# A decoder layer on one core: bf16 whole-number products in the expert listing, an unscaled turn of the second norm's rows, 41 expert steps in another order, and a third expert loaded early

## The chip, the cores and the metric

One core of one Trainium2 chip runs the whole layer. The metric is the device time of one execution in microseconds (us); the time of a kernel is the median of its runs. Engines: TensorE (PE; its weight loads are PEld), VectorE (DVE), ScalarE (ACT), GpSimd (POOL), SyncE (SP, which issues most DMAs). TensorE's granted clock is given as a share of 2.4 GHz.

## The reference

512 positions, width 1024, one layer. An attention part makes `h` (512 x 1024); then a mixture of experts is added:

```python
h = h + moe_ffn(rmsnorm(h, g_ffn), w_router, router_bias, w_gate, w_up, w_down, ws_gate, ws_up, ws_down)
# moe_ffn: scores = sigmoid(xf @ w_router); sel = scores + router_bias
#  the best 4 of 8 groups, then the best 8 of 64 experts by sel; w = scores of these, normalised, x 2.5
#  y[token] += w * ((silu(x @ w_gate[e]) * (x @ w_up[e])) @ w_down[e]) for each of its 8 experts
#  + (silu(xf @ ws_gate) * (xf @ ws_up)) @ ws_down      (the shared expert)
```

There are 64 experts with hidden width 256, so an expert's gate and up matrices are 2 MB in fp32 and its down matrix is 1 MB. 4096 (token, expert) pairs are computed. A gated embedding and a last norm follow. All tensors are fp32.

## The kernel before

Each engine has its own instruction stream, with semaphores between them written out by hand. The stages are `front_*` (input projection and attention), `middle_*` (merging, output projection, second norm, router, lists of rows), `experts_*` (the steps), `overflow_*` (a loop that runs only if an expert has more rows than its place) and `tail_*`.

**Middle.** TensorE makes the output projection in quarters of 256 columns for four tiles of 128 positions (`out_proj(t, q)`, L1100). When tile t's second half is added to `h` (L1278, counted by `h_done`), VectorE makes the sum of squares (`norm_sums`), GpSimd the power -0.5 (`rr`), and VectorE the normalised rows `y` (L1282, `xn`). `y` goes to DRAM as `xn2_rows` for the experts' gathers (L1024), and TensorE turns it (`transpose_xn`, L1111); VectorE and ScalarE each evict one half to `xn2T` (L1285, L1235). The router's products (L1119) and the shared expert's gate/up products (`shared_up`, L1125, eight of 512 columns a tile) read `xn2T`. ScalarE makes the scores (L1237). VectorE picks groups and experts (L1291 to L1328) and gives `mask`; then `wn`, the weights.

**Listing.** TensorE counts rows per expert with products of `mask` and ones (L1162, L1164), turns mask and weights (L1167, L1171), sorts experts by count with a permutation matrix (L1176, L1177, L1180), and gives each row its place by products with a triangle and ones (L1186) and an offset (L1191). All of these are fp32. The results are whole numbers, save the weights'. The weights are split into three bf16 parts by ScalarE and GpSimd in turns (L1245, L1248, L1043). `list_rows` (L963) are bf16 products of a one-hot matrix with a table `tokw`, which give each step's 128 row numbers and weights. Shared-expert products are put between these as filling.

**Steps.** Experts 0, 1 and 2 are fixed as ranks 0 to 2, so that they can be loaded before the order is known; the other ranks are sorted by row count. A step has 128 rows and is one of three kinds: F is one expert with 128 rows (`NFULL` of them, capacity 128); a trio T is two steps for two experts with 96 rows each and a third one with 32 rows in each; P is a pair with 64 rows each. The string `UNITS` gives their order; 42 steps. Step s on TensorE: gate/up products (L1484, 7 us), turning the next step's gathered rows (L1474), a list (L963), in the first steps one or two shared down products (L1071), the down products of step s-1 (L1508), and turning its own hidden rows (L1491). GpSimd gathers the rows of a step from DRAM and scatters its results.

**Loads.** There are six slots for experts' weights. `load_order` is ranks 0, 1, 2 and then the order of first use. A slot takes the next expert's gate/up as soon as the gate/up products of its holder's last step are done (semaphore `gu`), and its down matrix when the down products are done. The loads go out in SP's order (L1005, L1009). Before step 0, SP issues: experts 0 and 1 after the output projection, load 3 after the sorted `order`, gate/up of load 5, `w_shared_down`, and once all shared gate/up products are done, load 4, the rest of 5, and expert 2.

Of the kernel before, what the change touches and what calls it, by code (L numbers as in the profile page):

```python
# [21 lines left out]
BF16 = mybir.dt.bfloat16  # L22
ALU = mybir.AluOpType
# [26 lines left out]
NFULL = 6  # L50
NTRIO = 14
NPAIR = 8
# [52 lines left out]
def constants():  # L105
# [35 lines left out]
        ("cap_col", np.where(np.arange(P) % NE < NFULL, 128, np.where(np.arange(P) % NE < NFULL + 2 * NTRIO, 96, 64))[:, None]),  # L141
# [9 lines left out]
def build(nc, a, dbg=None):  # L151
# [8 lines left out]
    with ctx:  # L160
# [653 lines left out]
        wsg = sb("w_shared_up", X0, [P, 2, KD, EH])  # L814
# [4 lines left out]
        xpart = small[:, 96:104]  # L819

# [20 lines left out]
        UNITS = "FPPTTTPTFPTTTFTTFPPTPTTFPFTT"  # L841
        steps, n_full, n_trio, next_small = [], 0, 0, NFULL + 2 * NTRIO
        for u in UNITS:
            if u == "F":
                steps.append(full(n_full))
# [4 lines left out]
            else:  # L850
                steps += trio(NFULL + 2 * n_trio, NFULL + 2 * n_trio + 1, next_small)
# [13 lines left out]
        BUFFER = [2, 1, 0, 3, 4, 5]  # L865
        slot_of, landed_at, before, holder = {}, {}, {}, {}
        for x, r in enumerate(load_order):
# [3 lines left out]
            landed_at[r] = 16 + (landed_at[before[r]] if r in before else 0)  # L871
            slot_of[r], holder[v] = BUFFER[v], r

# [22 lines left out]
        sco, sel, selm, rep, mask, wn, pos1, smask = (wk(NT * NE, NT, NE) for _ in range(8))  # L896
# [5 lines left out]
        keys, above, perm = (wk(NE) for _ in range(3))  # L902
        own_key, my_rank = wk(1), wk(1)
        maskT, wnT = wk(NT * P, NT, P), wk(NT * P, NT, P)
# [10 lines left out]
        shared_in = {0: [(0, 0, 5), (0, 1, 6)], 1: [(1, 0, 7)], 2: [(1, 1, 7)], 3: [(2, 0, 7)], 4: [(2, 1, 7)], 5: [(3, 0, 7)], 6: [(3, 1, 7)]}  # L915
        shared_order = [v for i in range(7) for v in shared_in[i]]
# [15 lines left out]
        cn = ("sig merged_pe merged mt_hi mt_lo wo_done h_done ms rr xn stored xt_done xt_dve xt_act r_done listing_pe listing_act listing_dve listing_pool "  # L932
# [3 lines left out]
        for engine, done in (("pe", "counts maskT_pe wnT_pe sorted sorted_too pos_pe before_pe offs_pe"), ("act", "sco maskT wnT part0 part1 part2"),  # L936
                             ("pool", "rest0 rest1"), ("dve", "mask wn cnt_sb perm smask order over_pe over")):
# [73 lines left out]
        def middle_sync(sp):  # L1011
# [6 lines left out]
            for i, n in enumerate(("ws_gate", "ws_up")):  # L1018
                sp.dma_start(wsg[:, i], chunks(a[n][0])).then_inc(s_ws, 16)
# [41 lines left out]
        def shared_down(pe, t, i, b):  # L1061
# [6 lines left out]
            if n >= 2:  # L1068
# [1038 lines left out]
```

## Time and profile before

| | us |
|---|---|
| median of 3 runs | 1168.94 (1166.13 to 1172.79) |
| profiled execution | 1170.68 |
| its span | 1168.9 |
| TensorE busy | 1103.6 (94%) |
| VectorE busy | 462.8 (40%) |
| GB/s, mean over the span | 263 |

The span is the time from the first to the last instruction of the program. An idle stretch is put down to what ended it. Two records of TensorE belong to one fp32 product. The end of a matmul is modelled, so two records can overlap. A DMA's time to landing runs from its issue until all 16 of its parts have reported. All times below are us from the start of the span.

### The profile page before, as it was taken

To read this page: it belongs to the slowest core of one execution; us is meant where nothing else is said; L and a number is where in the kernel's file an instruction comes from. 1 tells how busy PE (TensorE), PEld (TensorE's weight loads), DVE (VectorE), ACT (ScalarE), POOL (GpSimd) and SP (SyncE) were. 2 spreads that over 40 slices of the span, in tenths; PEclk is the share of its full clock that TensorE was granted. 3 is DMA by queue.
4 is the path that set the end of the run, shared out by engine and by line. 5 is a ranking of instruction groups with operands and counts; after the bars stand their busy time and mean duration, and the time that the engine had idled before them with its cause. 6 is when DMAs were issued, how large, how long until landed. Compare 5 with 4: busy or idle time off the path is not lost.

```text
span 1168.9 us, 18877 instructions
## 1 busy us (share of the span) xinstructions
PE 1103.6 (94%) x7544; PEld 649.5 (56%) x7545; DVE 462.8 (40%) x1027; ACT 284.6 (24%) x642; POOL 283.4 (24%) x212
## 2 busy tenths in 40 slices
PE   6999999999998989999999999989998899998796
PEld 5888787767776879664333343334343333433375
DVE  5345655544546733542223422212221211111787
ACT  5023333333336410031111111111111111111623
POOL 3622524342333421010112112111111112110043
PEclk9999999999998989989999999999999999999899
DMA  9711212111112330669999999999999999988771
GB/s 365 266 37 37 73 55 73 54 55 55 55 38 104 130 119 37 250 235 411 404 424 414 424 425 427 421 419 421 412 422 417 427 399 421 425 360 316 321 313 72
DMA packets 51159, 307.77 MB, mean 263 GB/s; under 512 B 10368, under 2 KB 13312, under 8 KB 33152
## 3 DMA queue, kind: packets, MB, share of 16 engines
q1 hardware_dynamic: 38976, 272.99, 57.7%
q0 software_dynamic: 12096, 33.57, 7.2%
q8 instruction: 61, 1.00, 0.3%
q14 instruction: 26, 0.21, 0.0%
HBM read 290.80 MB, written 26.21 MB: 271 GB/s over the span
## 4 chain that ended last, share of the span: by engine, by line
PE 73%; DMA 16%; issue 5%; DVE 3%; POOLq 1%; POOL 1%; DVEq 0%; SPq 0%; ACT 0%
PE bank L1484 18%; PE bank L461 15%; DMA sb_gate_up<-in_w_gate_up 13%; PE bank L1508 8%; PE bank L1100 4%; PE bank L1090 4%; PE bank L470 3%; PE bank L494 3%; DMA sb_down<-in_w_down 3%; PE bank L525 3%; PE bank L1474 2%; PE bank L507 2%; PE bank L1125 2%; PE bank L1071 1%; PE bank L547 1%
## 5 line engine op out<-in xcount | busy, mean ns | idle before, releaser
L1484 PE MATMUL bank<-sb_gate_up,sb_xgT 128*32 128x512 f32 (+2 forms) x2144 | 301.8, 602 | 17.7 <-DMA sb_gate_up<-in_w_gate_up 17.7
L1484 PEld LDWEIGHTS bank<-sb_gate_up,sb_xgT 128*32 128x32 f32 (+2 forms) x2144 | 94.7, 118 | 192.7 <-issue 189.2
L461 PE MATMUL bank<-sb_x_hl,sb_w_hl 128*128 128x512 f32 x768 | 191.3, 401 | 10.6 <-DVE sb_x_hl L587 10.6
L461 PEld LDWEIGHTS bank<-sb_x_hl,sb_w_hl 128*128 128x128 f32 x768 | 141.7, 190 | 57.4 <-issue 24.5
L1508 PE MATMUL bank<-sb_down,sb_work 128*32 128x512 f32 (+2 forms) x1072 | 153.0, 595 | 3.9 <-DMA sb_down<-in_w_down 2.6
L1566 POOL DMA_INDIRECT expert_rows<-sb_rows_out,sb_work x42 | 43.6, 1037 | 455.3 <-DVE sb_rows_out L1644 455.3
L262 POOL TENSOR_TENSOR sb_w_hl<-sb_r,sb_w_hl 128x1024 fp32r<-128x1024 f32 x52 | 126.1, 2429 | 69.9 <-ACT sb_w_hl L1213 47.1
L1654 DVE TENSOR_TENSOR sb_work<-sb_work,bank 128x256 f32<-128x256 f32 x42 | 17.8, 423 | 269.4 <-ACT sb_work L1690 269.4
L1508 PEld LDWEIGHTS bank<-sb_down,sb_work 128*32 128x32 f32 (+2 forms) x1072 | 46.5, 116 | 80.3 <-issue 77.7
L1690 ACT ACTIVATE sb_work<-bank 128x256 f32<-128x256 f32 x42 | 16.2, 387 | 297.7 <-PE bank L1484 297.7
L671 DVE CUSTOM_DVE_ANT_0 sb_h<-bank,sb_bias 128x128 f32<-128x128 f32 (+3 forms) x96 | 43.4, 489 | 112.3 <-PE bank L494 111.7
L256 POOL CAST sb_w_hl<-sb_r 128x1024 fp32r<-128x1024 f32 x35 | 37.7, 1076 | 200.2 <-PE bank L461 157.6
L1644 DVE TENSOR_SCALAR sb_rows_out<-bank,sb_work 128x512 f32<-128x512 f32 x42 | 31.5, 751 | 134.9 <-PE bank L1508 134.9
L784 ACT ACTIVATE sb_h<-sb_h,sb_small 128x128 f32<-128x128 f32 (+3 forms) x96 | 53.3, 556 | 69.9 <-DVE sb_small L671 69.9
L1681 ACT ACTIVATE sb_rows_out<-bank,sb_work 128x512 f32<-128x512 f32 x42 | 28.9, 688 | 165.1 <-PE bank L1508 165.1
L794 ACT COPY sb_work<-bank 128x128 f32<-128x128 f32 (+4 forms) x104 | 40.5, 439 | 103.7 <-PE bank L507 92.9
L1474 PEld LDWEIGHTS bank<-sb_cst,sb_xg 128*128 128x128 f32 x336 | 41.0, 193 | 30.8 <-issue 29.1
L1100 PE MATMUL bank<-sb_w_hl,sb_m_hi 128*128 128x256 f32 x256 | 48.3, 291 | 4.8 <-DVE sb_m_lo L1258 4.8
L999 POOL DMA_INDIRECT sb_xg<-xn_rows,sb_work x42 | 43.4, 1033 | 37.9 <-PE bank L1474 16.4
L1474 PE MATMUL bank<-sb_cst,sb_xg 128*128 128x128 f32 x336 | 48.1, 286 | 0.0
L700 DVE TENSOR_SCALAR sb_h<-sb_h,sb_small 128x128 f32<-128x128 f32 (+3 forms) x96 | 43.3, 493 | 4.1 <-issue 0.4
L1100 PEld LDWEIGHTS bank<-sb_w_hl,sb_m_hi 128*128 128x128 f32 x256 | 41.3, 198 | 5.2 <-issue 5.2
(253 smaller groups left out, 1320.3 us busy)
## 6 DMA issues: line engine op xcount, KB each, us to landing
sb_gate_up<-in_w_gate_up SPq DMA_DIRECT2D x64, 2048.0 KB, 28.5
sb_down<-in_w_down SPq DMA_DIRECT2D x64, 1024.0 KB, 29.9
sb_r<-in_w_front SPq DMA_DIRECT2D x54, 512.0 KB, 3.5
sb_rows<-expert_rows SPq DMA_DIRECT2D x6, 2048.0 KB, 16.3
sb_gateT<-in_cmp_w SPq DMA_DIRECT2D x2, 2048.0 KB, 13.4
sb_rows<-expert_rows SPq DMA_DIRECT2D x3, 1024.0 KB, 8.5
sb_y<-in_x_T SPq DMA_DIRECT2D x4, 512.0 KB, 7.5
sb_h<-in_x SPq DMA_DIRECT2D x4, 512.0 KB, 11.1
```

The lines of the kernel that those rows point to most:

```text
L262: nc.gpsimd.tensor_tensor(w6_hl[:, slot, 1], raw_at[buf], w6_hl[:, slot, 0].bitcast(F32), ALU.subtract).then_inc(s_split, 1)
L461: last = nc.tensor.matmul(out[:, :], w6_hl[:, slot_at[n], zw, k, :], x_hl[:, zx, k, :], start=k + i == 0, stop=k == KD - 1 and i == 2)
L671: nc.vector.tensor_tensor_reduce(out=sc[:, i % 3, hh, 0:n_of(u)], in0=bank[BS[hh]][:, 0:n_of(u)], in1=bias[:, u["pair"] % 2, hh, S - n_of( ...
L700: nc.vector.tensor_scalar(sc[:, i % 3, hh, 0:n_of(u)], sc[:, i % 3, hh, 0:n_of(u)], c[:, hh:hh + 1], None, ALU.mult).then_inc(F["scaled"], 1)
L784: nc.scalar.activation(sc[:, i % 3, hh, 0:n_of(u)], sc[:, i % 3, hh, 0:n_of(u)], ACT.Exp, scale=-1.0, bias=minus_max[:, i % 4, hh:hh + 1], ...
L999: nc.gpsimd.indirect_dma_start(out=xg[s % 2], out_offset=None, in_=xn2_d, in_offset=bass.IndirectOffsetOnAxis(ap=idx[:, s:s + 1], axis=0), ...
L1090: last = nc.tensor.matmul(bank[2 * (m % 4) + i][:, :], w6_hl[:, SLOT_OF[m], zw, k, :], x_hl[:, zx, k, :], start=k % 4 + j == 0, stop=k % 4 ...
L1100: last = nc.tensor.matmul(bank[t][:, (q % 2) * 256:(q % 2 + 1) * 256], part_of_m, w6_hl[:, lo:lo + 2, zw, k, :], start=k + i == 0, stop=k ...
L1474: last = nc.tensor.transpose(bank[BX[half]][:, (k % 4) * P:(k % 4 + 1) * P], rows[:, k, :], ident)
L1484: last = nc.tensor.matmul(bank[BH][rows, :], xgT[:, k, rows], gate_up[slot_of[r]][:, :, k, :], start=k == 0, stop=k == KD - 1)
L1508: last = nc.tensor.matmul(bank[BO[i]][rows, :], hT[:, c, rows], Wd[slot_of[r]][:, c, i * 512:(i + 1) * 512], start=c == 0, stop=c == 1)
L1566: nc.gpsimd.indirect_dma_start(out=rows_d, out_offset=bass.IndirectOffsetOnAxis(ap=dst[:, s:s + 1], axis=0), in_=osb[s % 2], in_offset=Non ...
```

## The change

1. **bf16 for whole numbers.** `mask`, `smask`, `maskT`, `above`, `perm16`, `ones16`, `tri16`, `ident16`, `e_col16` are bf16; the products and the mask's transposes that read only these are bf16. `perm` stays in fp32 beside it for the weights and counts.
2. **Rows turned unscaled.** TensorE turns `h` instead of `y` (`transpose_h`), and one place earlier: after `out_proj(t + 1, 2)`. The gain `g_ffn` is multiplied in at the eviction, by columns (`g2_col`); the row factor `xpart` comes in later, as the scale of the sigmoid (now one operation per tile), of the shared SiLU, and of the product with the up half. The last tile's router product goes to a bank of its own. `y` is still made and stored for the gathers. The order of the shared products changes, and the copies to `tokw` move ahead of the residual adds. `ws_gate` and `ws_up` are one array, interleaved by chunk.
3. **Steps.** NFULL 1, NTRIO 17, NPAIR 6: 41 steps. The fixed experts have 96 rows in trios. The one expert with 128 rows is rank 3. The order begins T, P, P, P, P.
4. **Loads.** Expert 2 is loaded after the last W_out piece is split, ahead of the stores of the normalised rows. Loads 4 and 5 have their slots where `w_shared_up` and `xn2T` lie, and their gate/up weights come in two halves. One shared down product a step, in steps 0 to 7, all in bank 7.

```diff
-NFULL = 6
-NTRIO = 14
-NPAIR = 8
+NFULL = 1
+NTRIO = 17
+NPAIR = 6
+BIGGEST = NPRE
...
-        UNITS = "FPPTTTPTFPTTTFTTFPPTPTTFPFTT"
+        UNITS = "TPPPPTTTTTTTTTTPTTPTTFTT"
+        members = [r for r in range(NFULL + 2 * NTRIO) if r != BIGGEST]
...
-        BUFFER = [2, 1, 0, 3, 4, 5]
+        BUFFER = [1, 2, 3, 5, 0, 4]
+        IN_HALVES = (4, 5)
...
-        shared_in = {0: [(0, 0, 5), (0, 1, 6)], 1: [(1, 0, 7)], 2: [(1, 1, 7)], 3: [(2, 0, 7)], 4: [(2, 1, 7)], 5: [(3, 0, 7)], 6: [(3, 1, 7)]}
+        shared_in = {s: [(s // 2, s % 2, 7)] for s in range(2 * NT)}
...
             sp.dma_start(wsd[1][:, :], a["ws_down"][0, P:2 * P, :]).then_inc(s_wsd, 16)
+            sp.wait_ge(s_split, WO_PIECE + KD)
+            load_gate_up(sp, 2, 2)
+            load_down(sp, 2, 2)
...
-            def transpose_xn(t):
-                pe.wait_ge(M["xn"], t + 1)
+            def transpose_h(t):
+                pe.wait_ge(M["h_done"], NT + t + 1)
...
                 out_proj(t, 2)
+                if t:
+                    transpose_h(t - 1)
...
                 out_proj(t, 3)
-                if t:
-                    transpose_xn(t - 1)
-            pe.wait_ge(M["h_done"], NT + 1)
-            pe.wait_ge(s_ws, 32)
-            shared_up(0)
-            transpose_xn(3)
             router(2)
+            transpose_h(3)
+            pe.wait_ge(s_ws, 16)
+            shared_up(0, range(1))
             router(3)
+            shared_up(0, range(1, KD))
             pe.wait_ge(M["h_done"], 2 * NT)
-            shared_up(1)
-            shared_up(2, range(3))
+
+            others = [(t, k) for k in range(4) for t in range(1, NT)]
+            for t, k in others[:3]:
+                shared_up(t, (k,))
...
-                nc.tensor.matmul(bank[7][0:NE, 0:P], mask[:, t, :], C["ones"], start=t == 0, stop=t == NT - 1)
...
+                nc.tensor.matmul(bank[7][0:NE, 0:P], mask[:, t, :], ones16, start=t == 0, stop=t == NT - 1)
...
-                    last = nc.tensor.matmul(bank[6][:, t * NE:(t + 1) * NE], C["tri"] if v == t else C["ones"],
+                    last = nc.tensor.matmul(bank[6][:, t * NE:(t + 1) * NE], tri16 if v == t else ones16,
...
-            shared_up(2, range(3, 6))
+            for t, k in others[3:8]:
+                shared_up(t, (k,))
...
-            shared_up(2, range(6, KD))
-            shared_up(3)
+            for t, k in others[8:]:
+                shared_up(t, (k,))
+            for t in range(1, NT):
+                shared_up(t, range(4, KD))
...
-                nc.scalar.copy(xn2T[:, 4:8, t * P:(t + 1) * P], psv(5, 4, P)).then_inc(M["xt_act"], 1)
...
+                for k in range(4, KD):
+                    last = nc.scalar.activation(xn2T[:, k, t * P:(t + 1) * P], psv(5, 4, P)[:, k - 4, :], ACT.Copy, scale=g2_col[:, k:k + 1])
+                last.then_inc(M["xt_act"], 1)
...
-            sp.wait_ge(s_split, WO_PIECE + KD)
+            def half_of_gate_up(x, i):
+                slot = slot_of[load_order[x]]
+                sp.dma_start(raw[slot][:, i, :], a["w_gate_up"][expert[x]][:, 2048 * i:2048 * (i + 1)]).then_inc(s_raw[slot], 16)
+
+            sp.wait_ge(M["stored"], 16 * NT)
+            sp.wait_ge(M["xt_done"], NT)
             sp.wait_ge(*LISTING["order"])
             number(3)
             load_gate_up(sp, expert[3], load_order[3])
...
+            for x in IN_HALVES:
+                number(x)
+                load_down(sp, expert[x], load_order[x])
+            sp.wait_ge(M["gu_half"], 1)
+            for x in IN_HALVES:
+                half_of_gate_up(x, 0)
             sp.wait_ge(E["list"], 4)
             sp.dma_start(wsd[0][:, :], a["ws_down"][0, 0:P, :]).then_inc(s_wsd, 16)
+            load_down(sp, expert[3], load_order[3])
             sp.wait_ge(M["gu_done"], NT)
...
+            for x in IN_HALVES:
+                half_of_gate_up(x, 1)
```

## Rows read from the trace of the kernel before

**Rows 1.** The page's part 4: shares of the chain that ended last, by engine.

```profile
PE 73%; DMA 16%; issue 5%; DVE 3%; POOLq 1%; POOL 1%; DVEq 0%; SPq 0%; ACT 0%
```

**Rows 2.** Timeline of TensorE, 474 to 528: start, duration, line, form, records, [idle before].

```profile
474.41 7.03 PE L1125 MATMUL bank<-sb_w_shared_up,sb_gateT 128*128 128x512 f32 x16
...
482.15 3.68 PE L1119 MATMUL bank<-sb_gateT 128*128 128x64 f32 x32
...
495.50 1.09 PE L1162 MATMUL bank<-sb_cst,sb_work 128*64 128x128 f32 x8 [0.17 <-DVE sb_work L1328]
...
502.20 4.53 PE L1186 MATMUL bank<-sb_work,sb_cst 128*128 128x64 f32 x20
506.66 1.97 PE L1191 MATMUL bank<-sb_work 64*128 64x64 f32 x8
508.56 4.28 PE L1125 MATMUL bank<-sb_w_shared_up,sb_gateT 128*128 128x512 f32 x6
512.67 0.47 PE L963 MATMUL bank<-sb_work 128*128 128x6 bf16 x12
...
514.67 8.85 PE L1125 MATMUL bank<-sb_w_shared_up,sb_gateT 128*128 128x512 f32 x20
...
527.41 7.13 PE L1484 MATMUL bank<-sb_gate_up,sb_xgT 128*128 128x512 f32 x16
```

**Rows 3.** Windows: length, busy by engine, clock, DMA share, GB/s; sum over 474.40:527.40.

```profile
495.40:501.60 6.20, 5.41 (x43) 4.67 (x43) 3.60 (x15) 1.06 (x2) 0.00 (x0) 0.97 0.22 91
501.60:510.75 9.15, 9.15 (x34) 7.55 (x34) 3.26 (x6) 6.28 (x7) 1.70 (x2) 0.50 0.82 319
...
sum 53.00, PE 49.61 PEld 30.99 DVE 28.47 ACT 10.90 POOL 7.33; mean PE 6.20 PEld 3.87 DVE 3.56 ACT 1.36 POOL 0.92
...
552.40:1054.70 502.30, 481.52 (x3759) 187.31 (x3757) 112.60 (x249) 74.10 (x154) 79.43 (x77) 0.99 1.00 415
```

**Rows 4.** Waits of TensorE, 470 to 1100: total, times, longest.

```profile
PE bank L1484 <- DMA sb_gate_up<-in_w_gate_up: 17.7, 7, 4.0
...
PE bank L1508 <- DMA sb_down<-in_w_down: 2.6, 3, 1.3
```

**Rows 5.** The chain that ended last, in order of time: start, duration, what.

```profile
578.72 1.92 PE bank L1071 x4
...
627.13 7.00 PE bank L1484 x64
...
639.58 7.00 PE bank L1484 x64
...
1010.30 44.45 DMA sb_gate_up<-in_w_gate_up
...
1054.89 8.41 PE bank L1484 x64
```

**Rows 6.** Timeline of VectorE and ScalarE between scores and step 1.

```profile
486.29 0.43 DVE L1291 TENSOR_TENSOR sb_work<-sb_work,sb_gateT 128x256 f32<-128x256 f32 x1 [2.32 <-ACT sb_work L1237]
...
495.02 0.43 DVE L1328 TENSOR_TENSOR sb_work<-sb_work 128x256 f32<-128x256 f32 x1
...
507.21 1.36 ACT L1248 CAST sb_work<-sb_work 128x256 bf16<-128x256 f32 x1 [0.96 <-POOL sb_work L1043]
...
549.05 0.39 ACT L1690 ACTIVATE sb_work<-bank 128x256 f32<-128x256 f32 x1 [8.27 <-PE bank L1484]
```

**Rows 7.** Timeline of SP's queue: issues of expert loads.

```profile
502.13 0.35 SPq L1005 DMA_DIRECT2D sb_gate_up<-in_w_gate_up  x1
...
503.85 0.34 SPq L1005 DMA_DIRECT2D sb_gate_up<-in_w_gate_up  x1
...
534.72 0.35 SPq L1005 DMA_DIRECT2D sb_gate_up<-in_w_gate_up  x1
```

**Rows 8.** Line L1005: time to landing of the loads issued at 503.85 and at 534.72.

```profile
DMA to landing us min/median/max: 14.3/14.3/14.3
...
DMA to landing us min/median/max: 17.7/17.7/17.7
```

More of the change, by code:

```diff
@@ L819, in build @@
         xpart = small[:, 96:104]
+        g2_col = small[:, 436:436 + KD]
         m_hi = sb("m_hi", Y0, [P, NT, KD, P], F32R)
@@ L844, in build @@
             if u == "F":
-                steps.append(full(n_full))
+                steps.append(full(BIGGEST + n_full))
                 n_full += 1
@@ L850, in build @@
             else:
-                steps += trio(NFULL + 2 * n_trio, NFULL + 2 * n_trio + 1, next_small)
+                steps += trio(members[2 * n_trio], members[2 * n_trio + 1], next_small)
                 n_trio += 1
@@ L871, in build @@
             landed_at[r] = 16 + (landed_at[before[r]] if r in before else 0)
+            landed_gu[r] = (32 if x in IN_HALVES else 16) + (landed_gu[before[r]] if r in before else 0)
             slot_of[r], holder[v] = BUFFER[v], r
@@ L895, in build @@
         onehot_too = work[:, at_moe + NT * NE:at_moe + NT * NE + NT * CAP // 2].bitcast(BF16).rearrange("p (a b) -> p a b", a=NT)
-        sco, sel, selm, rep, mask, wn, pos1, smask = (wk(NT * NE, NT, NE) for _ in range(8))
+        sco, sel, selm, rep, wn, pos1 = (wk(NT * NE, NT, NE) for _ in range(6))
+        wk16 = lambda n: wk(n // 2).bitcast(BF16)
+        mask, smask = (wk16(NT * NE).rearrange("p (a b) -> p a b", a=NT) for _ in range(2))
+        ones16, tri16, ident16 = (wk16(P) for _ in range(3))
+        above, perm16, e_col16 = wk16(NE), wk16(NE), wk16(2)
         g8 = wk(NT * NG * 8, NT * NG, 8)
@@ L901, in build @@
         cnt_sb = wk(P)
-        keys, above, perm = (wk(NE) for _ in range(3))
+        keys, perm = (wk(NE) for _ in range(2))
         own_key, my_rank = wk(1), wk(1)
-        maskT, wnT = wk(NT * P, NT, P), wk(NT * P, NT, P)
+        wnT = wk(NT * P, NT, P)
+        maskT = wk16(NT * P).rearrange("p (a b) -> p a b", a=NT)
         assert at[0] <= WORK, at[0]
@@ L936, in build @@
         for engine, done in (("pe", "counts maskT_pe wnT_pe sorted sorted_too pos_pe before_pe offs_pe"), ("act", "sco maskT wnT part0 part1 part2"),
-                             ("pool", "rest0 rest1"), ("dve", "mask wn cnt_sb perm smask order over_pe over")):
+                             ("pool", "rest0 rest1"), ("dve", "mask wn cnt_sb perm perm32 smask order over_pe over")):
             for n, name in enumerate(done.split()):
@@ L1128, in shared_up @@
                     last.then_inc(M["gu_done"], 1)
+                elif (t, k) == (3, 3):
+                    last.then_inc(M["gu_half"], 1)
             pe.wait_ge(s_split, WO_PIECE + 4)
@@ L1232, in middle_scalar, with turned_rows @@
             round_piece(WO_PIECE + 7)
+            def turned_rows(t):
+                act.wait_ge(M["xt_done"], t + 1)
+                for k in range(4, KD):
+                    last = nc.scalar.activation(xn2T[:, k, t * P:(t + 1) * P], psv(5, 4, P)[:, k - 4, :], ACT.Copy, scale=g2_col[:, k:k + 1])
+                last.then_inc(M["xt_act"], 1)
+            act.wait_ge(s_g2, 32)
+            for t in range(NT - 1):
+                turned_rows(t)
+            turned_rows(NT - 1)
+            act.wait_ge(M["rr"], NT)
+            act.wait_ge(M["r_done"], NT - 1)
             for t in range(NT):
[L1234 to L1237 removed]
+                if t == NT - 1:
+                    act.wait_ge(M["r_done"], NT)
+                last = nc.scalar.activation(sco[:, t, :], router_out(t), ACT.Sigmoid, scale=xpart[:, 4 + t:5 + t])
+            last.then_inc(M["listing_act"], 1)
             act.wait_ge(*LISTING["maskT_pe"])
@@ L1271, in middle_vector @@
             dve.wait_ge(s_xagain, 16)
-            dve.wait_ge(s_g2, 16)
+            dve.wait_ge(s_g2, 32)
+            for v16, v in ((ones16, C["ones"]), (tri16, C["tri"]), (ident16, ident), (e_col16[:, 0:1], C["e_col"])):
+                nc.vector.tensor_copy(v16, v)
+            nc.vector.tensor_copy(tokw[:, :, :, 0], C["tok_a"].unsqueeze(1).to_broadcast([P, NE, NT]))
+            nc.vector.tensor_copy(tokw[:, :, :, 1], C["tok_b"].unsqueeze(1).to_broadcast([P, NE, NT]))
             for t in range(NT):
```

87 lines of the change are left out of this document (41 added, 46 removed).

## The prediction

> **What bounds the kernel now.** I read the page's shares first: TensorE is busy 94% of the span and 73% of the chain that ended last is its work, 16% is DMA [rows 1]. That average hides two stages. From about 474 to 527 us, routing and listing, the reader should see in TensorE's timeline one long file with small holes: whatever leaves it brings step 0 forward [rows 2]. From step 0 on the windows tell something else. Over 502 us the DMA engines have share 1.00 at 415 GB/s while TensorE is busy 481.52 of 502.30 [rows 3]. TensorE's waits in that stage are only 17.7 us for gate/up weights and 2.6 us for down weights [rows 4], so the two are nearly in step. Which one sets the end is told by the chain: the 63rd gate/up load is issued at 1010.30, lands 44.45 us later, at 1054.75, and step 40 begins 0.14 us after that [rows 5]. A load that lands 44 us after its issue stood in a queue; the 2 MB themselves take 5 us at 415 GB/s. So **the end is set by the stream of expert weights**: landing of load 63, then two steps and the tail, 1168.9 - 1054.75 = 114.2 us, none of which the change edits.
>
> The need of each kind of step says the same. One expert is 3.15 MB, and rows in and out are together 33.6 MB over 42 steps, 0.8 MB a step. Two steps of a trio (3 experts) need (9.44 + 1.6)/0.415 = 26.6 us of DMA against 2 x 12.45 = 24.9 us of TensorE; a pair step 17.1 against 12.45; a step of one full expert 9.5 against 12.45. All 64 experts and the rows: 235 MB/0.415 = 566 us of DMA, against 42 steps of TensorE = 42 x 12.45 + 8 x 1.8 = 537 us [rows 3, 5]. DMA is the longer by 29 us.
>
> **Change 1, 42 steps become 41.** One step is 12.45 us of TensorE (627.13 to 639.58) [rows 5]. The 4096 routed rows and 64 experts remain, so DMA has the same bytes. With the end set by the stream, this is worth **0**: TensorE waits 12 us more for weights. Were TensorE the bound it would be 12.4. I take 0, as the queue is 44 us long at the end. The last units are F, T, T in both orders, so load 63 still releases the last but one step. Going back from step 39: the F step waits for load 58, which is 5 experts and 3 steps' rows earlier, (15.7 + 2.4)/0.415 = 44 us against 37 us of steps, so load 63 decides; the trio before F waits for load 56, 63 us against 62, a tie; further back the stream's lead grows again. So at most a microsecond of the step's worth is near. For the capacities I counted the reference's routing on its own inputs: the fixed experts have 71, 56 and 67 rows (96 allowed), the largest other 102 (128), the next 88 (96), and from rank 35 on at most 62 (64). Nothing overflows.
>
> **Change 2, the listing.** TensorE ends the output projection at 474.4 and starts step 0 at 527.4, 53.0 us with 3.4 us idle [rows 2]. An fp32 product leaves two records. (a) Leaving TensorE: the counts (8 products, 2.0), the mask's transposes, the sorted mask (1.2), the positions (10 products, 4.5), the offsets (1.9). For bf16 the nearest row is the list product: 12 with 128x128 weights in 0.47 us, 0.04 each, but with 6 columns [rows 2]; with 64 and 128 columns I take 0.06. The same work then takes 0.45, 0.25, 0.3, 0.6, 0.3. Saved: 1.5 + 0.2 + 0.9 + 3.9 + 1.6 = **8.1** (bounds: 7 if each takes 0.1, 8.5). (b) Waits: the last tile's transposes need h alone. They no longer stand behind shared_up(0) (7 us), but behind router(2): begin 474.4 + 1.8, end 477.0; eviction with the gain, by VectorE in one operation as now, by ScalarE in four of 128x128 instead of one; its 128x256 form took 0.39 [rows 6], so 1.6 at most, 0.6 at least, 1.2 taken; router(3) until 480.1; scores at 480.5 instead of 486.3. From scores to mask is 9.2 us on VectorE (486.29 to 495.45), unchanged: mask at 489.7 [rows 2, 6]. TensorE has 8 + 3 shared products ahead of it, 9.5 us at 0.87, until 488.7. Its holes in the new order: before router(3) 0.5, before the mask 1.0, for the weights' transposes 1.3 (wn takes as long after the mask as before), for wnT 0.3, for the lists 1.1 (ScalarE's and GpSimd's three-part split of the weights now ends at 501.3: it ended at 508.57, and sorted_too comes 7.3 earlier) [rows 6], between lists 1.0, at step 0 1.5: 6.7, 3.3 more than before. (c) Clock: from 501.60 to 510.75 the granted clock is 0.50, the 1.2 GHz level, and three shared products take 4.28 us instead of 2.6 [rows 2, 3]. Without that dip, 53.0 - 8.1 + 3.3 - 1.7 = 46.5: step 0 at 520.9. With a dip of the same length over the listing, five shared products cost 4.3 more and the 1.1 hole is covered: 49.7, step 0 at 524.1. The stretch before the dip had short products with holes (5.41 busy of 6.20), and the new one has shorter ones with more holes [rows 3], so I lean to the dip: **step 0 at 523**, 4.4 us earlier.
>
> The Trainium skill, page "TensorE: Matmul & The Clock Gate", Part 1, says that half rate is the default and that sustained activity releases it. This speaks against turning products into shorter ones, and is the fourth case below. The dip in [rows 3] agrees with it in kind.
>
> What is added is covered: four casts and two copies to tokw on VectorE lie before 437 us, while it waits for the output projection; the scale in the shared hidden rows is an operand of operations that exist. If these covers failed it would be about 2 us.
>
> **Change 3, loads.** Expert 2 is loaded when the last W_out piece is split (about 440 us), 3.15 MB while DMA stands nearly idle; SP waits there anyway, until the first normalised rows. Experts 0 and 1 leave behind the last xn row's store as now, since that row is not earlier. Load 3 follows `order` (about 493), the halves of 4 and 5 at about 510 and 518. So at step 0 all six slots are full, where now three and a half are. But then nothing can be loaded until a slot frees. Load 7 goes 7.3 us into step 0 (534.72 now) [rows 7], loads 8 and 9 when step 1's gate/up products end, 21.6 us after the start of step 0 (549.05 - 527.41) [rows 2, 6]. One of two shared products leaves step 0 (-1.85 [rows 5]): **19.8 us**. From there on freed slots ask for 6.3 MB a step in four pair steps, 17 us of DMA in 14.2, so the queue doesn't run dry again.
>
> Now compare states. In the kernel before, load 7 lands at 534.72 + 17.7 = 552.4, and load 8 flows next [rows 7, 8]. After, load 8 flows at 523 + 19.8 + restart. The restart of an empty queue: 5.24 MB from 502.13 landed at 503.85 + 14.3 = 518.2, 16.0 us against 12.6 at 415 GB/s, so 3.4, part of which is completion that 552.4 also contains [rows 7, 8]. Between 0 and 3.4 I take 1.7. Load 8 flows at 544.5, **7.9 us earlier**, and all later loads with it, since bytes and rate are the same.
>
> The skill's page "DMA: Bandwidth & Descriptors", Anatomy of one DMA, gives about 2.0 us fixed per DMA, mostly completion. Our row shows 3.4; by the page's figure the estimate would hardly differ.
>
> **Sum.** Profiled execution 1170.68 us (span 1168.9). Step 0 earlier 4.4; step 0 shorter 1.85; load 7 no longer waited for 552.4 - (527.4 + 21.6) = 3.4; restart -1.7; step removed 0. Total 7.9: 1162.8. The median of the runs shown is 1168.94, 1.7 lower: **1161.0**. The bounds: step 0 at 521 and no restart cost, -11.6; step 0 unmoved and 3.4, -1.8: 1157 to 1167.
>
> **Rivals.** *The step counts too.* Start -4.4 and step -12.4: 1152. For it: TensorE busy nearly throughout and 20.3 us of weight waits in all [rows 3, 4]. Against it: share 1.00, and the chain's last wait. It needs load 63 to be 9 us earlier still, that is a stream 2% faster (9 of 502 us) than 415 GB/s; four pair steps at the start keep the queue deeper, which might do that. 0.13.
> *The loads pay, the listing doesn't* (other holes, or gathers late): step 0 at 527, 1166.5. 0.17.
> *The lighter listing holds the clock low* (the other side). If 1.2 GHz lasts from the mask to step 0, the 21 shared products left there cost 0.87 each more, 18 us: step 0 at 541, load 8 at 562.5 instead of 552.4, 10 later: 1179. It turns slower than before once step 0 starts after 530.9 (523 + 7.9). Against it: 0.50 ended by itself under three shared products [rows 2, 3]. 0.08.
> *It doesn't do what it says*: if the device's counts exceeded a capacity, each overflow block would load 3 MB and run serially, at least 8.6 + 12.4 us: 1182 and more. 0.02, by the counts above.
>
> **How the numbers follow.** Forecast 0.60, rivals 0.13, 0.17, 0.08, 0.02. The measurement can tell 0.5%, 5.8 us, from no change, which lies inside the forecast's own range (1157 to 1167): about 0.45 of its 0.60 is beyond it, with 0.13 of the first rival and 0.01 of the second 0.59 faster; same 0.15 + 0.16 = 0.31; slower 0.10. The range reaches from the first rival to a little above the second, 1151 to 1169.
>
> **What would show it.** Step 0's first gate/up product at 521 to 524; positions' products under 1 us; a clock dip near 496 to 506; SP's refill for load 8 at about 543; DMA share 1.00 from there and idle slices just before; load 63 landing near 1047; TensorE's waits for weights grown from 20 to about 30 us; the tail unchanged at 114. Wrong if weight waits shrink (then the step counted), or if DMA has idle slices after 560 us (slots, not bandwidth, bound).

## The result, and the profile after

The kernel after takes **1162.18 us** (median of 6 runs, 1159.71 to 1163.49), the kernel before 1170.05 on the same chip (6 runs, 1166.13 to 1172.79): ratio 0.993, 95% interval 0.9913 to 0.9948, 7.9 us less. The forecast was 1161.0. The profiled execution took 1159.71 us, the least of the six, with a span of 1157.9.

I read it in the order of the prediction: shares, TensorE between the output projection and step 0, SP's queue and DMA around the restart, waits, chain. The page's shares of the chain, for [rows 1]:

```profile
PE 70%; DMA 19%; issue 5%; DVE 3%; POOLq 1%; POOL 1%; DVEq 0%; SPq 0%; ACT 0%
```

DMA's share rose and TensorE's fell: the chain stands on loads longer than before. TensorE's timeline, for [rows 2] (start, duration, line, operation, records, idle time before and what ended it):

```profile
472.17 1.89 PE L1140 MATMUL bank<-sb_gateT 128*128 128x64 f32 x16
473.90 1.04 PE L1132 MATMUL bank<-sb_cst,sb_h 128*128 128x128 f32 x8
474.78 1.02 PE L1146 MATMUL bank<-sb_w_shared_up,sb_gateT 128*128 128x512 f32 x2
476.26 1.97 PE L1140 MATMUL bank<-sb_gateT 128*128 128x64 f32 x16 [0.46 <-ACT sb_gateT L1265]
478.07 8.80 PE L1146 MATMUL bank<-sb_w_shared_up,sb_gateT 128*128 128x512 f32 x20
487.54 0.41 PE L1187 MATMUL bank<-sb_work 128*64 128x128 bf16 x4 [0.67 <-DVE sb_work L1378]
...
493.30 0.72 PE L1212 MATMUL bank<-sb_work 128*128 128x64 bf16 x10
493.94 0.39 PE L1217 MATMUL bank<-sb_work 64*128 64x64 bf16 x4
494.27 6.77 PE L1146 MATMUL bank<-sb_w_shared_up,sb_gateT 128*128 128x512 f32 x10
...
503.07 14.00 PE L1146 MATMUL bank<-sb_w_shared_up,sb_gateT 128*128 128x512 f32 x32
...
520.73 0.30 PE L975 MATMUL bank<-sb_work 128*64 128x6 bf16 x8 [1.54 <-DVE sb_work L989]
520.96 7.07 PE L1536 MATMUL bank<-sb_gate_up,sb_xgT 128*32 128x512 f32 x64
```

The positions take 0.72 us where they took 4.53, the mask is turned at 487.5 instead of 495.5, and step 0 begins at 520.96 instead of 527.41. Of these 6.45 us, 2.2 lie ahead of routing and listing: the output projection with the third tile's turn was over at 472.17 in this execution (first line) and at 474.41 in the one before [rows 2]. From that point step 0 is 48.8 us away instead of 53.0. In the twelve variants profiled below, nearly all with the same work up to there, the projection ended between 472.0 and 475.8, so these 2.2 us can't be credited to the change, and I count from the projection wherever executions are compared.

The windows over the dip of the clock and over the restart, for [rows 3] (length, busy by engine, granted clock, DMA share, GB/s):

```profile
490.90:500.00 9.10, 9.07 (x37) 5.03 (x38) 5.60 (x13) 4.31 (x4) 2.07 (x2) 0.62 0.98 390
...
525.00:530.00 5.00, 5.00 (x67) 2.38 (x56) 1.09 (x4) 1.50 (x4) 0.00 (x0) 1.00 0.33 93
530.00:535.00 5.00, 3.68 (x50) 1.78 (x50) 2.87 (x12) 0.49 (x2) 0.99 (x1) 1.00 0.91 385
535.00:540.00 5.00, 5.00 (x52) 2.03 (x48) 0.58 (x2) 0.00 (x0) 0.00 (x0) 1.00 0.21 84
540.00:545.00 5.00, 5.00 (x64) 2.50 (x60) 1.70 (x4) 0.97 (x2) 0.00 (x0) 1.00 0.63 210
545.00:560.00 15.00, 15.00 (x106) 5.51 (x102) 3.13 (x6) 1.92 (x4) 2.17 (x2) 1.00 1.01 413
```

With all six slots full DMA has little to do from 525 to 541 but load 7 (the window from 530); it restarts when step 1's gate/up products end. ScalarE's SiLU of step 1, which follows them, and SP's queue (the last line holds load 7 at 528.24 and loads 8 and 9 at 541.0 and 542.1), for [rows 6] and [rows 7]:

```profile
540.86 0.38 ACT L1743 ACTIVATE sb_work<-bank 128x256 f32<-128x256 f32 x1 [8.14 <-PE bank L1536]
...
438.44 0.33 SPq L1017 DMA_DIRECT2D sb_gate_up<-in_w_gate_up  x1
...
528.24 14.20 SPq L1017 DMA_DIRECT2D sb_gate_up<-in_w_gate_up  x3
```

TensorE's waits for weights, for [rows 4] (total, times, longest), and the end of the chain, for [rows 5]:

```profile
PE bank L1536 <- DMA sb_gate_up<-in_w_gate_up: 17.9, 7, 4.3
...
PE bank L1560 <- DMA sb_down<-in_w_down: 3.1, 2, 1.7
```

```profile
1002.19 41.55 DMA sb_gate_up<-in_w_gate_up
1043.88 8.77 PE bank L1536 x64
```

Load 63 lands at 1043.74, 11.0 us earlier than in [rows 5], and the tail is unchanged: 1157.9 - 1043.74 = 114.2. All that is gained is gained before load 63 lands. Less the 2.2 us of the earlier projection, 8.8 of the 11.0 are left.

### The profile page after: what moved, and what is told of

Its sections match the earlier page's. It is cut to its first block, busy times and chain, and to the rows that moved or that the text cites. A ratio compares the mean times of both kernels' runs of the same rounds, so it can differ in the third digit from the quotient of the medians.

```text
span 1157.9 us, 19667 instructions
## 1 busy us (share of the span) xinstructions
PE 1090.7 (94%) x7927; PEld 632.2 (55%) x7928; DVE 462.6 (40%) x1032; ACT 285.4 (25%) x653; POOL 282.0 (24%) x210
## 3 DMA queue, kind: packets, MB, share of 16 engines
q0 software_dynamic: 11808, 33.57, 7.3%
q8 instruction: 64, 1.05, 0.3%
## 4 chain that ended last, share of the span: by engine, by line
PE 70%; DMA 19%; issue 5%; DVE 3%; POOLq 1%; POOL 1%; DVEq 0%; SPq 0%; ACT 0%
PE bank L1536 17%; PE bank L462 16%; DMA sb_gate_up<-in_w_gate_up 15%; PE bank L1560 7%; PE bank L1119 4%; PE bank L1109 4%; PE bank L471 3%; PE bank L495 3%; DMA sb_down<-in_w_down 3%; PE bank L526 3%; PE bank L508 2%; PE bank L1526 2%; PE bank L1146 2%; PE bank L1086 1%; PE bank L548 1%
## 5 line engine op out<-in xcount | busy, mean ns | idle before, releaser
L1536 PE MATMUL bank<-sb_gate_up,sb_xgT 128*32 128x512 f32 (+1 forms) x2384 | 298.1, 606 | 18.0 <-DMA sb_gate_up<-in_w_gate_up 17.9
L462 PE MATMUL bank<-sb_x_hl,sb_w_hl 128*128 128x512 f32 x768 | 191.8, 403 | 9.5 <-DVE sb_x_hl L588 9.5
L1536 PEld LDWEIGHTS bank<-sb_gate_up,sb_xgT 128*32 128x32 f32 (+1 forms) x2384 | 89.5, 115 | 195.0 <-issue 191.4
L1560 PE MATMUL bank<-sb_down,sb_work 128*32 128x512 f32 (+1 forms) x1192 | 149.3, 595 | 4.8 <-DMA sb_down<-in_w_down 3.1
L263 POOL TENSOR_TENSOR sb_w_hl<-sb_r,sb_w_hl 128x1024 fp32r<-128x1024 f32 x52 | 126.5, 2437 | 68.2 <-ACT sb_w_hl L1242 45.3
L1560 PEld LDWEIGHTS bank<-sb_down,sb_work 128*32 128x32 f32 (+1 forms) x1192 | 44.0, 112 | 81.7 <-issue 78.2
L1109 PE MATMUL bank<-sb_x_hl,sb_w_hl 128*128 128x512 f32 x192 | 43.9, 390 | 0.0
```

Of the source, the lines that this page charges most:

```text
L263: nc.gpsimd.tensor_tensor(w6_hl[:, slot, 1], raw_at[buf], w6_hl[:, slot, 0].bitcast(F32), ALU.subtract).then_inc(s_split, 1)
L462: last = nc.tensor.matmul(out[:, :], w6_hl[:, slot_at[n], zw, k, :], x_hl[:, zx, k, :], start=k + i == 0, stop=k == KD - 1 and i == 2)
L1109: last = nc.tensor.matmul(bank[2 * (m % 4) + i][:, :], w6_hl[:, SLOT_OF[m], zw, k, :], x_hl[:, zx, k, :], start=k % 4 + j == 0, stop=k % 4 ...
L1536: last = nc.tensor.matmul(bank[BH][rows, :], xgT[:, k, rows], gate_up[slot_of[r]][:, :, k, :], start=k == 0, stop=k == KD - 1)
L1560: last = nc.tensor.matmul(bank[BO[i]][rows, :], hT[:, c, rows], Wd[slot_of[r]][:, c, i * 512:(i + 1) * 512], start=c == 0, stop=c == 1)
```

## The experiments

One table holds what I read from each profile. "Projection": the start of the first instruction of TensorE behind it and the third tile's turn (where an expectation names a release of 68.6 or 66.8, it is counted from 0.1 us later). "Release": start of the SiLU of step 1, after which loads 8 and 9 may go, counted from the projection. "Stream": from the release to the landing of load 63 (in lists1, whose chain doesn't show it, the start of step 39's gate/up products, which waited for it, less 0.14). For the kernel before, the stream flows from the landing of load 7 at 552.4, and both columns are counted to and from there. steps44 and spread43 are not in it: the first has idle DMA within the stream, and in the second TensorE did not wait for load 63. The kernels were timed on several chips, each beside the kernel before. So differences are given twice: "by the medians" is the plain difference, "by the ratios" the difference of the ratios to before, times 1170.

| kernel | median us | ratio to before, 95% | projection | release | stream |
|---|---|---|---|---|---|
| before | 1170.05 | - | 474.4 | 78.0 | 502.3 |
| after | 1162.18 | 0.9913 to 0.9948 | 472.2 | 68.7 | 502.9 |
| fp32_listing | 1167.02 | 0.9955 to 0.9981 | 473.2 | 74.6 | 502.7 |
| turn_late | 1167.97 | 0.9972 to 0.9996 | 472.0 | 75.5 | 503.3 |
| fill8 | 1168.95 | 0.9982 to 1.0006 | 473.5 | 75.6 | 503.5 |
| late2 | 1162.68 | 0.9922 to 0.996 | 475.8 | 69.0 | 504.1 |
| skip6 | 1158.19 | 0.9879 to 0.9916 | 473.8 | 65.6 | 503.6 |
| shift_lists | 1159.94 | 0.9897 to 0.9931 | 473.6 | 66.1 | 503.6 |
| shift1 | 1160.23 | 0.9894 to 0.9921 | 474.1 | 66.4 | 503.9 |
| lists1 | 1161.95 | 0.9899 to 0.993 | 474.6 | 68.2 | 503.5 |
| steps42 | 1164.95 | 0.9947 to 0.9971 | 474.4 | 68.5 | 506.7 |
| spread42 | 1164.68 | 0.9939 to 0.9972 | 474.1 | 68.9 | 506.4 |

**Theory:** the stream of weights sets the end; its length from the release on is fixed for a given number of steps, and the change moves the release. **Rivals:** the step that is gone counts with its 12.4 us of TensorE; or the early load of expert 2 brings the gain.

### Does the release move the end?

fill8 puts eight more shared products ahead of step 0:

```diff
+            for k in range(4):
+                for t in range(2):
+                    nc.tensor.matmul(bank[6][:, :], xn2T[:, k, t * P:(t + 1) * P], wsg[:, k, :, :], start=True, stop=True)
```

> The changed kernel with eight shared-expert products more (into an unused bank, their result is not read) between the lists and the last shared products: TensorE's work ahead of step 0 is 6.9 us longer. Theory (step 0's start sets when slots come free, so the whole stream moves with it): step 0 starts 6.9 later, load 8 is issued 6.9 later and the end is 6 to 7 us later, ratio about 0.999. Rival (the stream has slack at its start): less than 2 us, ratio below 0.995.

The release came 6.9 us later (75.6 against 68.7) and the run took 6.8 us more by the medians, 7.5 by the ratios: one for one within the noise, with nothing absorbed in 500 us of steps.

skip6 leaves six shared products out:

```diff
-                shared_up(t, range(4, KD))
+                shared_up(t, range(4, 5))
+                shared_up(t, range(7, KD))
```

> The changed kernel without the products of chunks 5 and 6 of the shared expert's gate and up matrices for tiles 1, 2 and 3 (six products of TensorE, just ahead of step 0 are left out, so the shared expert's part of the result is not computed in full). Theory: TensorE's file sets step 0 even then, 5.2 us earlier, and the end 5 us earlier than the changed kernel, ratio 0.988 to 0.990. Rival (with the listing shortened, the lists and gathers now set step 0): gain under 2 us, ratio above 0.991.

4.0 us less by the medians, 3.9 by the ratios, so the direction holds, but the products are worth 5.25 (a shared product is 14.00/16 = 0.875 us). Step 0 did begin 4.8 us nearer to the projection (the missing half microsecond is the second fall described with lists1); then its gate/up products took 8.77 us instead of 7.07, and the release came 3.1 us earlier. The profiled execution is the slowest of the five (1160.23 us), so it isn't known whether the others lost this too. Timeline of TensorE and windows of skip6:

```profile
517.59 0.30 PE L975 MATMUL bank<-sb_work 128*64 128x6 bf16 x8 [1.54 <-DVE sb_work L989]
517.82 8.77 PE L1537 MATMUL bank<-sb_gate_up,sb_xgT 128*32 128x512 f32 x64
...
516.00:518.00 2.00, 0.46 (x13) 0.40 (x16) 1.44 (x4) 0.22 (x1) 1.15 (x1) 1.00 1.03 426
518.00:520.00 2.00, 2.00 (x12) 0.44 (x8) 0.69 (x2) 0.00 (x0) 0.00 (x0) 0.51 1.03 434
520.00:522.00 2.00, 2.00 (x16) 0.57 (x12) 0.00 (x0) 0.00 (x0) 0.00 (x0) 0.63 0.98 410
```

The granted clock fell to about 0.5, the 1.2 GHz level, just behind a stretch in which TensorE was busy 0.46 of 2.00 us. The Trainium skill, page "TensorE: Matmul & The Clock Gate", Part 1, says that sustained activity is what releases the clock; this fits in kind. The changed kernel has the same 1.54 us hole and no fall there, so the hole alone doesn't decide it, and what does stays open.

### Does a step count?

steps42 turns one trio unit (two steps, three experts) into three single full experts, side by side in the middle: 42 steps again, everything else as after.

```diff
-NFULL = 1
-NTRIO = 17
+NFULL = 4
+NTRIO = 16
...
-        UNITS = "TPPPPTTTTTTTTTTPTTPTTFTT"
+        UNITS = "TPPPPTTTTTFFFTTTTPTTPTTFTT"
```

> The changed kernel with one trio (two steps, three experts) in the middle replaced by three steps of one full expert each: 42 steps again, the same 64 experts and 4096 rows, the same loads before step 0. Theory (the stream of weights sets the end; a step is worth nothing): within 2 us of the changed kernel, ratio to the kernel before 0.993 to 0.995; TensorE's waits for weights fall by about 12 us, load 63 lands where it did. Rival (the step counts): 12.4 us slower than the changed kernel, ratio about 1.004.

2.8 us slower than after by the medians, 3.4 by the ratios: far from 12.4, and not zero.

steps44 does it three times, with nine single experts in a row (`NFULL = 10`, `NTRIO = 14`, `UNITS = "TPPPPTTTFFFFFFFFFTTTTPTTPTTFTT"`).

> The same with three trios replaced by nine full steps: 44 steps. The changed kernel's step pitches hold about 29 us beyond the plain 12.4 and 14.2, so three steps more (37 us) should use up all of it and a little more. Theory of the stream: 8 to 14 us slower than the changed kernel (ratio about 1.001 to 1.005), TensorE's waits near 0 to 5 us. Rival (each step counts): 37 us slower, ratio about 1.025.

1171.22 us, ratio 1.0016 (1.0003 to 1.0028), 9 to 10 us slower than after. Windows of steps44 over the nine:

```profile
720.00:760.00 40.00, 40.00 (x162) 19.94 (x161) 8.35 (x22) 5.75 (x12) 8.10 (x8) 1.00 0.96 382
760.00:800.00 40.00, 40.00 (x222) 19.24 (x221) 9.35 (x23) 6.72 (x14) 6.08 (x6) 1.00 0.94 351
800.00:840.00 40.00, 39.85 (x381) 14.99 (x383) 9.17 (x23) 6.68 (x14) 6.08 (x6) 1.00 0.97 389
```

Here TensorE is busy throughout and DMA isn't: a step of one expert frees its slot after 12.4 us and asks for 9.5 us of DMA. But TensorE's waits for gate/up weights fell to 7.0 us from 17.9, and yet the time rose. Half of it is this idle DMA, 0.13 x 40 = 5 us; the other half, 4 to 5 us, had no account yet.

That left two accounts of the same constant stream, which spread42 and spread43 tell apart. spread42 has steps42's three single experts set apart, where after waits for weights (`UNITS = "TPPPPTTTTTTTPTPFTTFTFTTFTT"`); spread43 has two more steps than after (`NFULL = 7`, `NTRIO = 15`, `UNITS = "TPPPPTTTTTTTTFTFTFPFTFTFPFTT"`).

> One trio unit turned into three single full experts, as in steps42, but the three are set apart (units 16, 19, 21) where TensorE waits for weights in the changed kernel (after 830 us), so that no slot is held while a load could use it. It separates two accounts of the constant 503 us from the release of loads 8 and 9 to the landing of load 63. If the bytes of the stream are the same for 42 steps (the queue's records give 33.57 MB of rows for 41, 42 and 44 steps) and steps42 lost its 3 us to idle DMA between its three neighbours, this one is as fast as the changed kernel: ratio 0.993 to 0.994, load 63 503 to 504 us after the release; the restart of the empty queue then cost some 0.4 us. If a step's rows cost the stream something (the memory counters on the page rise by 1.05 MB a step, 2.5 us at 415 GB/s), it is 1.5 to 2.5 us slower: 0.9945 to 0.9955, load 63 at 505 to 506; the restart then cost 2 to 3 us and hid it in the sum. The step's TensorE time, 12.4 us (1.004), is the third case.

> The same doubled: two more steps than the changed kernel, six more full experts, all after about 800 us and none beside another. Weight waits as read from the pitches of the steps are 29 us in the changed kernel and two steps need 24.9. Same bytes: ratio 0.993 to 0.995 (a microsecond or two where the waits are not where the steps come). A step's rows cost 1.5 to 2.5 us each: 3 to 5 us slower, 0.996 to 0.9975. TensorE's time counts: 25 us, 1.014.

spread42: 1164.68 us, 2.5 slower than after by the medians, 3.0 by the ratios, as slow as steps42 although its single experts stand apart, and load 63 again lands 506.4 us after the release. spread43: 1167.09 us, ratio 0.9979 (0.9969 to 0.999), 4.9 slower by the medians, 5.7 by the ratios. So **a step costs some 3 us of stream** (2.5 to 3.4 by the times), and no less where the single experts stand apart. Against the nine kernels with 41 steps, whose streams are 502.7 to 504.1 us and 503.5 in the mean, the streams of steps42 and spread42 are longer by 3.2 and 2.9. spread43 is the weaker witness, as TensorE no longer waits for its load 63. The other half of steps44's loss, 4 to 5 us for three steps, is less than three times 3; this rest stays open. The page's DMA part of after, then of spread42:

```profile
q0 software_dynamic: 11808, 33.57, 7.3%
...
HBM read 290.28 MB, written 25.69 MB: 273 GB/s over the span
```

```profile
q0 software_dynamic: 12096, 33.57, 7.3%
...
HBM read 290.81 MB, written 26.21 MB: 273 GB/s over the span
```

The records of the gathers' and scatters' queue hold 33.57 MB whether there are 41, 42, 43 or 44 steps: 4096 rows of 4 KB in and as many out are 33.55, so a step's empty lanes move no row. Yet each step adds 288 packets, and 0.52 MB read and 0.52 written in the memory counters, 1.05 MB, which at 415 GB/s are 2.5 us. The windows over the stream say the same: DMA share 1.00 in each, but 418, 416 and 415 GB/s for 41, 42 and 43 steps (after, spread42, spread43; the first two are shown).

```profile
545.00:1040.00 495.00, 475.11 (x4074) 178.30 (x4070) 110.06 (x248) 71.02 (x148) 76.30 (x74) 0.99 1.00 418
```

```profile
545.00:1045.00 500.00, 486.30 (x3956) 185.81 (x3958) 112.47 (x250) 73.03 (x152) 78.30 (x76) 0.99 1.00 416
```

(The first is after, the second spread42.) Whether it is the packets or unseen bytes that cost, no run separates.

### What of the listing?

fp32_listing computes the whole-number products in fp32 again:

```diff
-        ones16, tri16, ident16 = (wk16(P) for _ in range(3))
-        above, perm16, e_col16 = wk16(NE), wk16(NE), wk16(2)
+        ones16, tri16, ident16, e_col16 = C["ones"], C["tri"], ident, C["e_col"]
...
-        maskT = wk16(NT * P).rearrange("p (a b) -> p a b", a=NT)
+        maskT, wnT = wk(NT * P, NT, P), wk(NT * P, NT, P)
```

> The changed kernel with the listing's whole-number products, operands and mask transposes back in fp32; everything else as changed. TensorE's work ahead of step 0 grows by the 8 us estimated for them; about 1 us of it falls into holes (before the weights' transposes). Theory (step 0's start moves the end one for one): step 0 and the end 6 to 8 us later than in the changed kernel, ratio 0.998 to 1.000. Rival (the products were hidden beside VectorE's chain): under 3 us, ratio under 0.996.

It was less than expected: 4.8 us by the medians, 4.4 by the ratios. In the profile the release is 5.9 us later.

```profile
495.14 4.53 PE L1210 MATMUL bank<-sb_work,sb_cst 128*128 128x64 f32 x20
499.60 1.97 PE L1215 MATMUL bank<-sb_work 64*128 64x64 f32 x8
501.50 6.43 PE L1144 MATMUL bank<-sb_w_shared_up,sb_gateT 128*128 128x512 f32 x10
```

From the first count to the last offset TensorE is busy 12.0 us where in after it is 5.0, 7.0 more; its holes from the projection to step 0 are 4.8 us instead of 5.6, since long products cover VectorE's work; and the five shared products behind take 6.43 instead of 6.77. 7.0 - 0.8 - 0.3 = 5.9. So of the 7.0 us that bf16 takes from TensorE 0.8 come back as holes.

turn_late has the last turn wait for the scaled row again and puts it where it was, behind `shared_up(0)`:

```diff
-                pe.wait_ge(M["h_done"], NT + t + 1)
+                pe.wait_ge(M["xn"], t + 1)
...
-            router(2)
-            transpose_h(3)
...
+            shared_up(0)
+            transpose_h(3)
+            router(2)
```

> The changed kernel with the turning of the rows waiting for the normalised rows again, and with the old place in TensorE's order: after out_proj(t, 3), the last tile after all eight products of shared_up(0), and only then router(2) and router(3). It still turns h, so the arithmetic is the changed one. The scores and the mask come about 6 us later, and only three shared products are left to fill that, so a hole of 5 to 6 us opens ahead of the mask. Theory: end 5 to 6 us later than the changed kernel, ratio 0.997 to 0.999. Rival (TensorE's sum of work alone sets step 0): within 1 us, ratio 0.993 to 0.995.

5.8 us slower by the medians, 6.3 by the ratios, in the expected range; in the profile the release is 6.8 later. Its timeline:

```profile
471.97 7.03 PE L1146 MATMUL bank<-sb_w_shared_up,sb_gateT 128*128 128x512 f32 x16
...
492.70 0.64 PE L1186 MATMUL bank<-sb_work 128*64 128x128 bf16 x4 [6.67 <-DVE sb_work L1377]
...
507.96 15.70 PE L1146 MATMUL bank<-sb_w_shared_up,sb_gateT 128*128 128x512 f32 x32
```

The expected hole is there, 6.67 us ahead of the mask. From the projection (first line) to step 0 TensorE's holes are 10.3 us instead of 5.6. The other 2.1 of the 6.8 us are the same products taking longer: the granted clock was 0.50 from 489 to 502.8, where in after it was from 492 to 498.4, and again from 509 to 513. The edit undoes the wait and the place in the order together; no run separates them.

The two parts undone one at a time cost 5.9 and 6.8 us at the release, while step 0 gained 4.2 in all. That is no contradiction: eleven shared products stand ahead of the mask where nineteen stood, 8 x 0.875 = 7 us less filling. With the early scores that is right; with late scores it is the hole of 6.67 us, which before was 0.17 [rows 2].

### The early load

late2 loads expert 2 behind the halves of experts 4 and 5 instead of at 438 us:

```diff
-            sp.wait_ge(s_split, WO_PIECE + KD)
-            load_gate_up(sp, 2, 2)
-            load_down(sp, 2, 2)
```

> The changed kernel with expert 2 loaded last before step 0, behind the second halves of loads 4 and 5, instead of at 440 us. Nothing else differs. The changed kernel's DMA engines stand mostly idle from 525 to 541 us because all six slots are full; the 3.15 MB (7.6 us) fit there. Theory: within 1.5 us of the changed kernel (ratio 0.992 to 0.995), the early load pays nothing by itself. Rival (each byte moved ahead of step 0 is won): 7.6 us slower, ratio about 1.000.

0.5 us slower by the medians, 1.3 by the ratios, release 0.3 later: the early load of expert 2 is worth nothing that can be told apart here, since DMA stands mostly idle between 525 and 541 in any case. It costs nothing either: the projection ended no earlier without it (475.8). Two other parts of the change have no run of their own: the loads of experts 4 and 5 ahead of step 0, and the new order of the units.

### Two edits at the restart

shift1 moves the shared expert's down half-tiles one step on, so that step 0 has none:

```diff
-        shared_in = {s: [(s // 2, s % 2, 7)] for s in range(2 * NT)}
-        shared_order = [v for s in range(2 * NT) for v in shared_in[s]]
+        shared_in = {s + 1: [(s // 2, s % 2, 7)] for s in range(2 * NT)}
+        shared_order = [v for s in range(2 * NT) for v in shared_in[s + 1]]
```

lists1 moves lists to later steps (`lists_in = {0: [4, 5], 1: [6, 7, 8], 2: [9, 10]}`), and shift_lists, run first, is both.

> A version beyond the change. Two edits in the changed kernel: the eight shared down products stand in steps 1 to 8 instead of 0 to 7, and lists 4 to 10 are spread as two in step 0 (none ahead of its gate/up products), three in step 1, two in step 2. The first shortens step 0 by 1.85 us, the second takes the 1.5 us hole and 0.2 us of list products from ahead of step 0. Theory (what counts is when step 1's gate/up products end and free two slots): load 8 issued 3.5 us earlier, the end 3 to 4 us earlier than the changed kernel, ratio 0.989 to 0.991. Rival (the moved work comes back where VectorE and TensorE pass each other in steps 1 and 2): no gain, ratio 0.993 or more.

> One of the two edits of shift_lists alone: the shared expert's down half-tiles go into steps 1 to 8 instead of 0 to 7. If the release of loads 8 and 9 (ScalarE's SiLU of step 1) moves the end one for one, step 0 loses a half-tile, 1.85 us: release 66.8 us after the end of the output projection instead of 68.6, ratio to before 0.9915, 1160.3 us. Rival: what shift_lists lost (1 to 2 us of its expected 3 to 4) was lost here, since step 1 then waits longer for its own gathered rows: release 68 or later, ratio 0.993, no difference from the changed kernel. The half-tile added to step 8 is to cost nothing, as the stream sets the end.

> The other edit of shift_lists alone: lists 4, 5 in step 0, 6 to 8 in step 1, 9 and 10 in step 2. Expected: nearly nothing from step 0 (the hole of 1.5 us before its first gate/up product waits for list 4, which stays where it is), at most 0.7 us from one list less in each of steps 0 and 1 (a list's products are 0.3 us of TensorE, and one hole of 1.3 us waits for VectorE's one-hot): ratio 0.9925 to 0.993. Rival: the holes before and in step 0 are VectorE's backlog of lists, and go: 1.5 to 2.5 us, ratio 0.991. If the clock's second fall of shift_lists (504 to 508) shows here and not in shift1, the lists cause it.

shift_lists brought 2.2 us (1.9 by the ratios) where I had expected 3 to 4. Apart: **shift1 2.0 us** by the medians and 2.6 by the ratios, release 2.3 earlier, as its theory had it (1.85) and a little more; lists1 0.2 by the medians, 1.8 by the ratios (the lowest and the highest of its six runs are 3.9 us apart), release 0.5 earlier. What the lists save ahead of step 0 (0.94 us of hole instead of 1.54) they take again in step 1, behind the release: from its SiLU to the next one 15.05 us instead of 14.34. lists1 and shift_lists had a second fall of the clock, at 504 to 508, under the last 16 shared products: timeline and window of lists1:

```profile
504.18 15.70 PE L1146 MATMUL bank<-sb_w_shared_up,sb_gateT 128*128 128x512 f32 x32
...
506.00:508.00 2.00, 2.00 (x4) 0.85 (x3) 0.00 (x0) 0.00 (x0) 1.50 (x2) 0.50 0.91 373
```

The 16 products took 15.70 us instead of 14.00. The same 15.70 stands in turn_late, late2, spread42 and steps44, and in skip6 the ten that are left took 10.55 instead of 8.75; after, fp32_listing, fill8, shift1, steps42 and spread43 have no second fall. Up to this point TensorE gets the same instructions in after, late2, shift1, lists1, shift_lists and the four kernels with other steps, so none of these edits is its cause; what is stays open.

Nor is 1.7 us the price of having two falls. Where the second comes, the first is shorter: its five shared products took 5.57 to 5.73 us and not 5.94 to 7.20. From the projection to step 0, where the instructions are the same, after, shift1, steps42 and spread43 need 48.6 to 48.8 us with one fall, and late2, spread42 and steps44 49.0 to 49.1 with two: 0.2 to 0.5 us more.

shift1 and shift_lists ran some 2 us faster than after. That is about the width of the intervals, which overlap with after's; the release, 2.3 and 2.6 us earlier in the profiles, says the same.

## Why the prediction was right, step by step

The forecast was 7.9 us, the measurement 7.9. By the forecast's own terms, from the projection to the landing of load 63, the profiles give 8.8 (580.3 against 571.6 us); the ratio's interval, 6 to 10 us, holds both. That the totals agree to a tenth is luck. The forecast in us, 1161.0, is 1.2 low, as it was taken off the median of three runs, 1168.94; the median of six is 1170.05.

- **Step 0 earlier, 4.4:** 4.2 measured (53.0 to 48.8). Inside it two sizes were off and cancelled. bf16 saves 7.0 us of products (fp32_listing) and not 8.1. The holes are 5.6, as worked out for the case with a dip (6.7 less the covered 1.1). The dip came over the listing, as I leaned, but at 492 to 498.4 instead of 496 to 506, and its five shared products took 6.77 us, 2.4 over the full-rate price and not 4.3.
- **Step 0 shorter, 1.85:** 1.75 (start of step 0 to the release 21.64 us before, 19.90 after). shift1 repeated it with the other half-tile.
- **Load 7 no longer waited for, 3.4:** 3.4 (552.42 less 549.05). The release, not a load in flight, starts the stream now.
- **Restart, -1.7, and the step removed, 0:** these two failed as sizes and hid each other, by luck. Their sum is -0.55: the stream takes 502.9 us from the release and took 502.3 from the landing of load 7. I had written that DMA has the same bytes with one step less. By the queue's records it has, but steps42, spread42 and spread43 show some 3 us a step (2.5 to 3.4). So the step removed gave about 3, and the restart of the empty queue took 0.55 more than that, 3 to 4, at or above the upper end of the range of 0 to 3.4 that I had from [rows 7, 8]. The restart I only get as this difference, so whatever the new order of the units does to the stream is in it. The 2.0 us of the Trainium skill, page "DMA: Bandwidth & Descriptors", Anatomy of one DMA, is a fit for DMAs that GpSimd issues. The loads here are SP's, so it was no support for 1.7.
- **The stream sets the end:** fill8 and skip6 show it from both sides, and *the step counts too* (1152) is out: steps42 costs 3 and not 12.4.
- *The loads pay, the listing doesn't* is out in its second half: step 0 moved, and fp32_listing and turn_late lose 4 to 6 us. Its first half is true in part: the 3.4 of load 7 belongs to the loads ahead of step 0. late2 takes only expert 2's away and loses nothing clear; no run puts those of 4 and 5 back.
- *The lighter listing holds the clock low* did not happen in full. Shorter falls did, whose price is in the two paragraphs on lists1: a second one in seven variants, 0.2 to 0.5 us, and one at skip6's step 0, 1.7.

Of the signs announced, the restart came at 541 and not 543, load 63 at 1043.7 and not 1047 (most of both is the earlier projection, 2.2 us). One sign was badly chosen: I expected TensorE's weight waits to grow to 30 us, and the view of waits says 21.0. It counts only the time in which TensorE stood fully idle. By the pitches of the steps, read at the SiLU of each (14.25 us with a shared half-tile, 12.45 without), after spends some 29 us more than its work, before 24.

## What to carry over

Where a queue of loads is busy from some point to the end, find what releases its first load and count each edit by how far it moves that point; work removed behind it is worth only its DMA. When units are merged, price the fixed cost of their gathers and scatters by the time, not by the bytes of the records. When products are shortened, look at what they covered, and move filling along with them.

## What the runs showed of the hardware

- One step more, with its gather and its scatter, costs the stream some 3 us (2.5 to 3.4) although it moves no more rows: 288 packets, no more recorded bytes, 1.05 MB more in the memory counters (steps42, spread42, spread43).
- The granted clock fell to 0.50 at different places under the same TensorE instructions (after 492 to 498.4; lists1 at 495 to 498 and at 505 to 509; steps42 only at 493 to 499), the first time behind short products with holes, in turn_late within a hole of 6.67 us. A second fall added 1.7 us to the 16 products under it, but only 0.2 to 0.5 to the way from the projection to step 0.
- Ten whole-number products with 128x128 weights and 64 columns take 0.72 us in bf16 (after), the same in fp32 4.53 us (fp32_listing), with the clock at about half for both.
